# One pass over the mixer weights for token blocks 2 and 3 of the first layer

## What is computed

```python
# first layer, mixer
q, k, v, u, vg = split(h @ w_in)                 # q, k: RMS norm and rotary; v, k over 768 keys
a = rms_norm(diff_attend(q, k, v, lam)) * gain
g = u * (sgu_w @ layer_norm(vg) + sgu_b)         # within one block of 128 tokens
x = x + g1 * (concat(a, g) @ w_out)
# every layer, feed-forward (peer_ffn)
s = (h2 @ wq) . keys; two top-16 lists, 256 sums, top 16 of them, softmax gives gate
x = x + g2 * sum_k gate_k * gelu(w_down[idx_k] . h2) * w_up[idx_k]
```

## Time and profile before

| | |
|---|---|
| median of three runs | 3224.82 us |
| lowest, highest | 3224.18, 3225.63 us |
| span of the profiled execution (the page gives no other time of it) | 3226.1 us |
| loads of a weight chunk through line 791 | 70 |
| moved by DMA | 1286.05 MB |
| busy share: PE, DVE, ACT, POOL | 73%, 69%, 40%, 37% |

### The profile page before, as it was taken

One profiled execution on the slowest core, in us unless ns is written; L12 is line 12 of the kernel. 1 busy time (PEld: TensorE's weight loads), 2 busy tenths in 40 slices (PEclk: granted clock), 3 DMA queues, 4 the chain that ended last, 5 costly groups with the idle time before them and its releaser, 6 DMA issues.

```text
span 3226.1 us, 38561 instructions
## 1 busy us (share of the span) xinstructions
PE 2352.4 (73%) x13032; PEld 919.0 (28%) x13032; DVE 2215.5 (69%) x5652; ACT 1284.6 (40%) x3707; POOL 1194.8 (37%) x1076
## 2 busy tenths in 40 slices
PE   6997778576775878876685796956686667867776
PEld 2335225122341235431151251511143112511110
DVE  2325875866568655869849968599948996795444
ACT  3223463345434553533434534333343433443333
POOL 1102343433334342335433434335433453344332
PEclk9998789688887888887797796967688667966666
DMA  8778999999999999999999999999999999999998
GB/s 333 260 300 344 415 375 423 410 398 406 410 422 414 418 401 421 391 422 410 419 404 416 401 418 420 392 404 397 421 399 421 405 421 391 421 399 422 421 421 357
DMA packets 169766, 1286.05 MB, mean 399 GB/s; under 512 B 19552, under 2 KB 20448, under 8 KB 23392
## 3 DMA queue, kind: packets, MB, share of 16 engines
q0 software_dynamic: 154368, 1124.14, 85.4%
q1 hardware_dynamic: 15200, 159.45, 11.9%
HBM read 1281.42 MB, written 2.10 MB: 398 GB/s over the span
## 4 chain that ended last, share of the span: by engine, by line
DMA 33%; PE 31%; DVE 20%; ACT 8%; issue 7%; POOL 1%; DVEq 0%; SPq 0%; ACTq 0%; POOLq 0%
DMA ring<-in_experts,expert 32%; PE psum L1798 11%; DVE ring L1500 8%; PE psum L1564 7%; PE psum L1578 4%; PE psum L1744 4%; DVE arena L1391 2%; PE psum L1536 1%; PE psum L1595 1%; ACT shares_of L1128 1%; ACT diag L1129 1%; DVE arena L1419 1%; PE psum L1550 1%; ACT acts L1127 1%; ACT L1127 1%
## 5 line engine op out<-in xcount | busy, mean ns | idle before, releaser
L1798 PE MATMUL psum<-ring,diag 64*64 64x512 f32 x8192 | 1430.3, 805 | 746.7 <-ACT diag L1129 739.8
L852 POOL DMA_INDIRECT ring<-in_experts,expert x1024 | 1169.0, 1142 | 1807.0 <-PE psum L1798 1666.0
L1500 DVE CUSTOM_DVE_ANT_0 ring<-ring,h 128x1024 f32<-128x1024 f32 x1024 | 1230.9, 1223 | 530.3 <-DMA ring<-in_experts,expert 499.9
L1127 ACT ACTIVATE acts<-dots 128x1 f32<-128x1 f32 x1024 | 206.7, 202 | 1475.0 <-DVE dots L1500 1431.4
L1798 PEld LDWEIGHTS psum<-ring,diag 64*64 64x64 f32 x8192 | 286.4, 162 | 1719.5 <-ACT diag L1129 1519.6
L1129 ACT ACTIVATE diag<-ident_half,shares_of 128x64 f32<-128x64 f32 x1024 | 356.4, 348 | 33.3
L1128 ACT ACTIVATE shares_of<-acts,gate 128x1 f32<-128x1 f32 x1024 | 302.0, 295 | 33.3
L1391 DVE SCALAR_TENSOR_TENSOR arena<-kept,taps,arena 128x128 f32<-128x128 f32 x960 | 262.6, 345 | 0.1
L1578 PEld LDWEIGHTS psum<-arena,weights 128*128 128x128 f32 x2048 | 234.2, 192 | 48.9 <-issue 47.0
L1578 PE MATMUL psum<-arena,weights 128*128 128x128 f32 x2048 | 245.7, 278 | 0.1
L878 ACT ACTIVATE arena<-psum 128x512 f32<-128x512 f32 (+1 forms) x105 | 65.5, 624 | 206.0 <-PE psum L1578 119.6
(11 more groups left out here) (166 smaller groups left out, 1519.3 us busy)
## 6 DMA issues: line engine op xcount, KB each, us to landing
weights<-in_chunks SPq DMA_DIRECT2D x70, 2048.0 KB
ring<-in_chunks POOLq DMA_DIRECT2D x46, 1024.0 KB, 7.2
ring<-in_experts,expert POOLq DMA_INDIRECT x1024
arena<-in_chunks SPq DMA_DIRECT2D x10, 512.0 KB
x<-in_x SPq DMA_DIRECT2D x1, 2048.0 KB, 19.8
kept<-in_chunks POOLq DMA_DIRECT2D x2, 1024.0 KB, 19.9
out_x<-x SPq DMA_DIRECT2D x4, 512.0 KB
ring<-in_ctx SPq DMA_DIRECT2D x1, 1024.0 KB, 9.6
```

What stands on the lines that cost most here:

```text
L852: pool.indirect_dma_start(out=ring[:, k, :], out_offset=None, in_=table, in_offset=bass.IndirectOffsetOnAxis(ap=expert[:, s.b % 2, n:n + 1 ...
L1127: step(act.activation(acts[:, k:k + 1], dots[:, k:k + 1], ACT.Gelu))
L1500: dve.tensor_tensor_reduce(out=ring[:, k, 0:D], in0=ring[:, k, 0:D], in1=h2[:, s.b % 2, :], scale=1.0, scalar=0.0, op0=ALU.mult, op1=ALU.a ...
L1798: pe.matmul(ffn_out[rows_out, r * COLS:(r + 1) * COLS], diag[rows_in, k, :], ring[rows_in, k, D + n * COLS:D + (n + 1) * COLS], start=Fals ...
```

## The change

The mixers of blocks 2 and 3 both stand beside block 1's gathers. Block 3's stages are twins of block 2's: they read the same chunk while it is in its buffer, so a chunk of the mixer is loaded once for both. The pairs of stages that read a chunk are interleaved (`TWO_EVEN`, capital letters for block 3), except that block 3's attention comes behind block 2's projection. Block 3's normalized input, its q and its gating output get places of their own. ScalarE gets two new waits, one before it writes block 3's u (until block 2's gating output is there) and one before block 3's first exponentials (until block 2's `project` has updated x). The selections of blocks 2 and 3 stay where they were, beside block 1's and block 2's gathers. One memset of the convolution's padding moves to a later call.

```diff
-    def read(self, chunk, first, last, tile, part):
-        self.needs.setdefault(first, []).append(chunk)
+    def read(self, chunk, first, last, tile, part, again=False):
+        if not again:
+            self.needs.setdefault(first, []).append(chunk)
         self.dones.setdefault(last, []).append(chunk)
...
-        s.chunk = self.chunk(source)
+        s.twin = twin
+        s.chunk = twin.chunk if twin else self.chunk(source)
...
-EVEN = """
-n0 n1 n2 q0 q1 g0 q2 g1 q3 q4 g2 g3 q5 a0 a1 a2 a3 g4 a4 a5 a6 a7 a8 a9 a10 a11 a12 a13 a14 a15 a16 p0 a17 a18 p1 a19 a20 p2 a21 a22
-p3 p4 p5
+TWO_EVEN = """
+n0 n1 n2 N0 N1 N2 q0 q1 q2 q3 q4 Q0 q5 Q1 Q2 g0 Q3 g1 Q4 g2 Q5 g3 g4 G0 G1 G2 G3 a0 G4 a1 a2 a3 a4 a5 a6 a7 a8 a9 a10 a11 a12 a13 a14
+a15 a16 p0 a17 a18 p1 a19 a20 p2 a21 a22 p3 p4 p5 A0 A1 A2 A3 A4 A5 A6 A7 A8 A9 A10 A11 A12 A13 A14 A15 A16 P0 A17 A18 P1 A19 A20 P2
+A21 A22 P3 P4 P5
 """
...
-    def even(b):
-        return written(mixer(b), EVEN)
+    def two(b):
+
+        n, late_n = [p.norm(("x", b + i), None, out, (0, SH1)) for i, out in enumerate((("one", 0), ("late", 0)))]
+        q = p.heads("q", [b + CTX // P], Q_CH)
+        late_q = p.heads("q", [b + 1 + CTX // P], Q_CH, twin=q)
+        g = p.gating(b)
+        late_g = p.gating(b + 1, twin=g)
+        a, o = p.attend(b, p.so_far("topk_ready")), p.project(b, "even")
+        late_a = p.attend(b + 1, p.so_far("topk_ready"), twin=a)
+        late_o = p.project(b + 1, "even", twin=o)
+        order = written({"n": n, "N": late_n, "q": q, "Q": late_q, "g": g, "G": late_g, "a": a, "A": late_a, "p": o, "P": late_o}, TWO_EVEN)
+        return order + ffn_prep(0, b)
...
-    p.beside(0, 1, [lambda: even(2), lambda: ffn_prep(0, 2)])
-    p.beside(0, 2, [lambda: even(3), lambda: select_and_pointwise(0, 3, 0)])
+    p.beside(0, 1, [lambda: two(2)])
+    p.beside(0, 2, [lambda: select_and_pointwise(0, 3, 0)])
...
+                if s.twin:
+
+                    act.wait_ge(S["mixed_ready"], s.mixed_before)
                 evacuate(gated(s)[0], s.ut, tile_ap(s.ut, 512), "u_ready")
...
+                    if h == 0 and s.twin:
+
+                        act.wait_ge(S["x_updated"], s.x_updates)
```

More of the change, by code:

```diff
@@ L245, in norm, with heads @@
         return s
-    def heads(self, name, tiles, source, first=False):
+    def heads(self, name, tiles, source, first=False, twin=None):
         s = Stage("heads", name=name, tiles=tiles, first=first,
@@ L257, in heads @@
             s.claim(5 if name == "q" else 2 * n + (3 if n + 1 < len(tiles) else 2), s.turn[n])
-        s.read(s.chunk, 0, 2 * len(tiles) - 1, s.proj[-1], 0)
+        s.read(s.chunk, 0, 2 * len(tiles) - 1, s.proj[-1], 0, again=twin is not None)
         s.before, self.turned = self.turned, s.turn[-1]
@@ L275, in values, with gating @@
         return s
-    def gating(self, b, first=False):
+    def gating(self, b, first=False, twin=None):
         s = Stage("gating", b=b, first=first, cost=(1.3, 1.8, 1.3, 2.5, 2))
+        s.twin, s.mixed_before = twin, self.so_far("mixed_ready")
         s.ht, s.rotated = self.so_far("ht_ready"), self.so_far("qk_rotated")
-        s.vg, s.u = self.chunk(VG_CH), self.chunk(U_CH)
+        s.vg, s.u = (twin.vg, twin.u) if twin else (self.chunk(VG_CH), self.chunk(U_CH))
         s.ut, s.vt, s.mt = self.tile(), self.tile(), self.tile()
@@ L284, in gating @@
         s.claim(4, s.mt)
-        s.read(s.vg, 0, 1, s.vt, 0)
-        s.read(s.u, 2, 3, s.ut, 0)
+        s.read(s.vg, 0, 1, s.vt, 0, again=twin is not None)
+        s.read(s.u, 2, 3, s.ut, 0, again=twin is not None)
         s.u_ready = self.take("u_ready")
@@ L292, in gating, with attend @@
         return s
-    def attend(self, b, seen=0):
+    def attend(self, b, seen=0, twin=None):
         s = Stage("attend", b=b, cost=tuple(ATTEND_COST[what] for what, h in ATTEND))
+        s.twin, s.x_updates = twin, self.so_far("x_updated")
         s.qkt, s.v = self.so_far("qkt_ready"), self.so_far("v_ready")
@@ L315, in attend, with project @@
         return s
-    def project(self, b, which):
+    def project(self, b, which, twin=None):
         s = Stage("project", b=b, which=which, cost=(1, 1.3, 1.3, 1.5, 1.3, 2.5) if which == "even" else (2.5, 1.3, 1.3, 2.5))
@@ L321, in project @@
         s.tile = self.tile(2)
-        s.chunks = [self.chunk((OUT_CH if which == "even" else PW2_CH) + j) for j in range(2)]
+        s.twin = twin
+        s.chunks = twin.chunks if twin else [self.chunk((OUT_CH if which == "even" else PW2_CH) + j) for j in range(2)]
         s.left_before = self.so_far("left_ready")
@@ L330, in project @@
             for j in range(2):
-                s.read(s.chunks[j], 1 + j, 4 + j, s.tile, j)
+                s.read(s.chunks[j], 1 + j, 4 + j, s.tile, j, again=twin is not None)
             s.left = self.take("left_ready", 2)
@@ L628, in trunk_kernel @@
         vn_gain = sb("vn_gain", [P, 2, COLS])
+        late_mixed = sb("late_mixed", [P, COLS])
         neg_lam = sb("neg_lam", [P, 1])
@@ L684, in trunk_kernel @@
         q_t = at(2048, 512).rearrange("p (h n) -> p h n", h=HEADS)
+        late_q_t = at(7424, 512).rearrange("p (h n) -> p h n", h=HEADS)
+        late_h_t = at(4096, 1024).rearrange("p (k n) -> p k n", k=KD)
         qk_raw, qk_sq, qk_rot = at(2560, 512), at(3072, 512), at(3584, 512)
@@ L749, in modulated, with mixed_of @@
         def modulated(s):
-            return h_pair[:, :, s.out_t[1] * P:(s.out_t[1] + 1) * P] if s.out_t[0] == "pair" else h_t
+            if s.out_t[0] == "pair":
+                return h_pair[:, :, s.out_t[1] * P:(s.out_t[1] + 1) * P]
+            return {"one": h_t, "late": late_h_t}[s.out_t[0]]
+        def mixed_of(s):
+            return late_mixed[:] if s.twin else cat[:, HEADS * VD:]
         def gated(s):
@@ L970, in turned @@
                     tok = s.tiles[n]
-                    dst = k_t[:, :, tok * P:(tok + 1) * P] if s.name == "k" else q_t
+                    dst = k_t[:, :, tok * P:(tok + 1) * P] if s.name == "k" else late_q_t if s.twin else q_t
                     evacuate(dst, s.turn[n], tile_ap(s.turn[n], 512).rearrange("p (h n) -> p h n", h=HEADS), "qkt_ready")
@@ L1302, in gating @@
                     cols = slice(g * P, (g + 1) * P)
-                    issue(dve.scalar_tensor_tensor(out=cat[:, HEADS * VD + g * P:HEADS * VD + (g + 1) * P],
+                    issue(dve.scalar_tensor_tensor(out=mixed_of(s)[:, cols],
                                                    in0=tile_ap(t, 512)[:, cols], scalar=sgu_bias[:, g:g + 1],
@@ L1362, in conv_in @@
                     dve.memset(z_t[:, :, 0:PAD], 0.0)
+                else:
                     dve.memset(z_t[:, :, PAD + SEQ:], 0.0)
@@ L1650, in heads @@
                         pe.wait_ge(S["odd_ready"] if s.tiles[n] % 2 else S["even_ready"], s.tiles[n] // 2 + 1)
-                    yield from linear(s.proj[n], 0, ht_all[:, s.tiles[n]] if s.name == "k" or s.first else h_t, s.chunk)
+                    yield from linear(s.proj[n], 0, ht_all[:, s.tiles[n]] if s.name == "k" or s.first else late_h_t if s.twin else h_t, s.chunk)
                     if n:
@@ L1666, in gating @@
             def gating(s):
-                left = ht_all[:, CTX // P] if s.first else h_t
+                left = ht_all[:, CTX // P] if s.first else late_h_t if s.twin else h_t
                 vn = gated(s)[1]
@@ L1683, in attend @@
                 pe.wait_ge(S["qkt_ready"], s.qkt)
+                queries = late_q_t if s.twin else q_t
                 def score(h):
@@ L1690, in score @@
                         for lo, hi in ((0, COLS), (COLS, KEYS)):
-                            pe.matmul(psum[:, t.bank, lo:hi], q_t[r, h, :], k_t[r, h, lo:hi], start=True, stop=True).then_inc(
+                            pe.matmul(psum[:, t.bank, lo:hi], queries[r, h, :], k_t[r, h, lo:hi], start=True, stop=True).then_inc(
                                 full[t.bank], 1)
@@ L1718, in project @@
                             pe.wait_ge(S["cat_ready"], s.cat)
-                        turn(s.turn[part], cat[:, 512 * part:512 * part + 512], 4)
+                        turn(s.turn[part], mixed_of(s) if part else cat[:, 0:HEADS * VD], 4)
                         yield
```

## The result

The changed kernel takes 3248.76 us (median of 4 runs, 3245.03 to 3252.06), 1.0072 times before (95% interval 1.0058 to 1.0086), which took 3224.5 us in the runs beside it: 24 us slower, where 3217.2 was forecast. Its profiled execution has a span of 3246.1 us.

A forecast was written before the change was run, and what follows sets the result against it. DMA was taken to bound nearly all the time; -24.9 (bytes) - 5.7 (block 3's selection loss) + 13 (selection) + 7 (attention) + 3 (norms, linears) = -7.6 us, giving 3217.2 us, whole range 3201 to 3237.

The forecast's parts named there:

- Bytes: Five chunks no longer loaded for block 3, 10.49 MB less: 24.9 us saved at 421 GB/s, taken in full.
- The cover: Time in which DMA already stands idle, where saved loads are worth nothing: at most 2 to 4% in these stretches.
- (a): Selection beside block 1: VectorE sets the pace at 3.5 us a slot; +13 us, bounds +8 to +20.
- (c): Norms, q, gating and the selection's linears beside block 1: TensorE work about equals DMA; +3 us, between 0 and 10.
- (b): Attention beside block 1: heads 12.9 us each where DMA needs 11.7; +7 us, bounds 0 to +28.
- a line through mean periods: Attention heads: 18.35 us at 7.12 slots and 15.98 at 6.06 give 2.24 us a slot, so 12.9 at 4.68.
- The attention floor: Rival, chance 0.20: a chain over three engines keeps heads from going below 16.0 us; 3231 to 3239 us.
- The wash: Rival, chance 0.22: beside block 1, TensorE waits for selection chunks that land late; 3222 to 3230 us.
- The signs: Borders near 1078 and 1442 us, block 2's selection VectorE-bound at 330 to 360 GB/s, heads 12.9 to 13.5 us apart.
- the three signs of being wrong: Heads staying at 15 to 16 us, VectorE idling in the selection for weights, or 420 GB/s in both.

The follow-up runs named there:

- number 1: Changed kernel, but block 3's stages load their own chunks again (70 loads): 3253.9 us, ratio 1.0091 to the kernel before.
- number 5: Changed kernel with Relu in place of Gelu in block 1's gathers, sparing table loads: 3227.21 us, ratio 1.0001 to the kernel before.
- numbers 7 and 12: Changed kernel with VectorE's and ScalarE's phases one and two slots later behind TensorE's, beside block 1: 3241.11 us and 3235.78 us.
- the control: Kernel before with Relu in place of Gelu in block 1's gathers: 3223.23 us, ratio 0.999.
- number 11: Changed kernel with Relu in block 1's gathers, project's half-linear phases at weight 4.0, one slot more lag beside block 1: 3222.58 us, ratio 0.9986.

## Why the prediction was wrong

- **Bytes.** 65 loads and 1275.56 MB, as said. No run gives the five loads the 34 us that the prediction estimated by the Trainium skill ("DMA: Bandwidth & Descriptors", section "Anatomy of one DMA — SWDGE (gpsimd) path"); the fit there is for GpSimd's path, and these loads are SyncE's. The price of 24.9 us held in the sum only because block 2's stretch, from which the loads vanish, is at the DMA ceiling: 32.6 us less, 34 forecast. Sharing the chunks beside block 1 was worth nothing (number 1). The cover that I named, "at most the 2 to 4%", was that of the stretches before; the change itself made a cover of 63 us (429.1 less the 366 us that DMA needs for 154 MB).
- **(a) The selection's pieces** were right in mechanism and near in size: 11.0 us lost in the window against 14.3 reckoned, VectorE 92% busy there.
- **(c) Norms, q, gating, linears**: 9.3 us lost in 680 to 780, against 2 before (413 GB/s in the same window): +7, forecast +3, within the bounds.
- **(b) Attention is the step that failed.** It was sized at +7 and with it 16 us lost in all (the 9.0 of before and 7). Measured are 42.3 us. Two things are in that. First the heads, 20.6 us lost. I drew a line through mean periods, as if each step held 8.3 of weight. The steps are unlike: before, they hold 6, 6 and 7 slots beside block 1 and 5, 5 and 6 beside block 2 (there 14.3, 15.5 and 18.1 us long), after the change 3, 4 and 5. The last step, the one with all five phases of a head in it, took 18.15 us with 7 slots, 18.05 with 6, and now 17.6 and 16.9 with 5. It hardly fell with the density, so "no sign of a floor" was wrong. But it isn't a fixed cost of a head either: without ScalarE's table loads (number 5) it is 13.6 us, and with more lag (numbers 7 and 12) 14.6 and 12.5. The means were 14.2 and 13.8 us where 12.9 was forecast. Second the tails, 21.7 us lost. The line held nothing of `squares` to `p5`, where VectorE waits 9.1 and 7.7 us in the first tail.
- **The rivals.** The attention floor, at 0.20, was nearest: a chain over the engines did set the pace. But a head did go below its 16.0 us, and its price, without the tails, gave 3231 to 3239 and not 3249. The wash (weights late) has next to no share: between 950 and 1106 us TensorE's matmuls wait once for a weight chunk, 1.2 us, and its weight loads once, 2.1 us; in the rest of block 1's stretch neither does. The Trainium skill ("DMA: Bandwidth & Descriptors", section "SWDGE vs HWDGE vs iDMA") lets the queues take turns, which gave an estimate of 10 us; the trace is near it, with a median of 11.6 us from issue to landing on the page after.
- **The signs.** Predicted borders 1078 and 1442, measured 1106.0 and 1470.7. In the selection the signs came nearly as said (VectorE 92% busy where nearly 100% was named, 344 GB/s), as did block 2's 421 GB/s. None of the three signs of being wrong came: heads didn't stay at 15 to 16 us, VectorE hardly idled for weights in the selection, and block 1's stretch wasn't at 420 GB/s. The signs watched the heads and not the tails.

How the excess splits by cause cannot be given as a sum, since the edits overlap: off the stretch of 429.1 us the table loads take 21 us (17 over the control), the lag 13.5 with one slot and 18.0 with two, the tails' weights or TensorE work 6 to 8 (not clear of noise in the time), the three of number 11 together 31.1 with the selection 5 us worse. That the heads' last steps are a loop over the engines is argued from the waits; what was shown is that leaving out ScalarE's table loads or lengthening the lag shortens it. One rival was not tested: TensorE's granted clock in the heads' windows is 0.78 and 0.72 after and 0.80 and 0.83 before, so its own part of the chain takes a little longer as well.

## What to carry to other kernels

Work that hides under a DMA stream has a density above which it no longer hides (block 1's stretch took 373.5, 383.9 and 429.1 us with 1.17, 1.37 and 1.78 of weight a slot and the same number of bytes), and bytes saved there are worth nothing until the waits are gone (0 us and 11 us for the same 10.49 MB). Price moved work not by each engine's busy time alone but also by the dependence chains between two instructions of the engine that keeps the stream going, and do it for every part that moves, the tail of a stage too. Before drawing a line through mean periods, look at the single steps and count what each of them holds. Before sharing a load, check that its place is at the bandwidth ceiling in the new order, too.

## What was not expected of the hardware

A table load of 1.28 us on an engine that is 49% busy cost more than anything else that a single edit took away: 46.4 us less of ScalarE's time shortened the stretch by 21.0 us. Weight chunks of 2.1 MB landed in a median of 11.6 us after their issue, 181 GB/s, 43% of the 421 that the gathers reach alone.
